# Sources of the output projections transposed in 32x32 blocks by VectorE and reloaded through HBM, TensorE keeping the last ones

## The reference

```python
z = jnp.einsum('btd,de->bte', h, w_in)            # 1024 -> 8192: rq rk rv rg dq dk dv gr gd
y_r = einsum('btv,vd->btd', silu(rg) * rmsnorm(o_ret, g_ret), w_ret_o)
y_d = einsum('btv,vd->btd', rmsnorm(o_att, g_sub) * (1 - lam_init), w_diff_o)
m = sigmoid(gr) * y_r + sigmoid(gd) * y_d
x = x + einsum('btd,de->bte', m, w_out)
x = x + hier_moe(rmsnorm(x, g_ffn), ...)          # 16 experts, 2 per row
```

## Time and profile before

| | |
|---|---|
| median of 3 runs | 1011.21 us (1010.29 to 1013.48) |
| profiled execution | 1012.54 us, its span 1010.4 us |
| PE busy | 990.2 us, 98% |
| DVE busy | 689.5 us, 68% |
| ACT busy | 509.1 us, 50% |
| granted clock of PE | 0.991 |
| transposes under L1834 | 160 |

### The profile page before, as it was taken

One profiled execution on the slowest core, in us unless ns is written; L12 is line 12 of the kernel. 1 busy time (PEld: TensorE's weight loads), 2 busy tenths in 40 slices (PEclk: granted clock), 3 DMA queues, 4 the chain that ended last, 5 costly groups with the idle time before them and its releaser, 6 DMA issues.

```text
span 1010.4 us, 12083 instructions
## 1 busy us (share of the span) xinstructions
PE 990.2 (98%) x4614; PEld 812.8 (80%) x4614; DVE 689.5 (68%) x1003; ACT 509.1 (50%) x680; POOL 149.7 (15%) x184
## 2 busy tenths in 40 slices
PE   9989999999999999999999999999999999999995
PEld 6878888887887888877878888889788888888884
DVE  6699886237656664443448457687889889888893
ACT  6523233335545553332352304554588687887782
POOL 1000001112120301221130000022012122121111
PEclk9999999999999999999999999998999999999998
DMA  9489888882551732553285245137899999999994
GB/s 350 138 250 316 236 222 227 270 247 101 195 192 69 262 114 77 194 204 127 97 299 186 104 152 228 69 127 281 337 401 403 381 404 391 393 405 380 404 397 80
DMA packets 125987, 245.27 MB, mean 243 GB/s; under 512 B 69072, under 2 KB 69376, under 8 KB 113600
## 3 DMA queue, kind: packets, MB, share of 16 engines
q1 hardware_dynamic: 105520, 172.51, 47.1%
q0 software_dynamic: 20112, 71.37, 21.2%
q10 hardware_dynamic: 288, 0.52, 0.1%
HBM read 203.07 MB, written 52.08 MB: 253 GB/s over the span
## 4 chain that ended last, share of the span: by engine, by line
PE 56%; issue 27%; DVE 6%; POOL 3%; SPq 2%; ACT 2%; DMA 1%; POOLq 0%; ACTq 0%; DVEq 0%
PE ps L478 14%; PE ps L480 14%; PE ps L479 14%; PE ps L1861 3%; PE ps L1862 3%; SPq L586 2%; PE ps L1834 2%; POOL x_exp L855 1%; PE ps L1896 1%; POOL out_y L866 1%; PE ps L2004 1%; PE ps L2020 1%; DVE w_lo L450 1%; PE ps L2011 1%; DMA v_tok<-out_v_new 1%
## 5 line engine op out<-in xcount | busy, mean ns | idle before, releaser
L478 PE MATMUL ps<-w_hi,s_hi 128*128 128x512 f32 x640 | 256.4, 401 | 3.1 <-DVE w_lo L414 2.6
L480 PE MATMUL ps<-w_lo,s_hi 128*128 128x512 f32 x640 | 250.3, 391 | 0.0
L479 PE MATMUL ps<-w_hi,s_lo 128*128 128x512 f32 x640 | 249.9, 390 | 0.0
L478 PEld LDWEIGHTS ps<-w_hi,s_hi 128*128 128x128 f32 x640 | 120.6, 188 | 29.2 <-issue 4.6
L479 PEld LDWEIGHTS ps<-w_hi,s_lo 128*128 128x128 f32 x640 | 120.7, 189 | 25.5 <-issue 1.0
L480 PEld LDWEIGHTS ps<-w_lo,s_hi 128*128 128x128 f32 x640 | 120.5, 188 | 25.6
L1013 ACT ACTIVATE stage<-ps,x_rstd 128x512 f32<-128x512 f32 x64 | 43.6, 688 | 150.8 <-PE ps L480 150.4
L414 DVE TENSOR_TENSOR w_lo<-raw,w_hi 128x2048 fp32r<-128x2048 f32 x40 | 91.6, 2290 | 32.2 <-ACT w_hi L409 31.9
L409 ACT CAST w_hi<-raw 128x2048 fp32r<-128x2048 f32 x40 | 76.1, 1908 | 12.0 <-DMA raw<-in_w_in 6.3
L450 DVE TENSOR_TENSOR lo_x<-raw_x,hi_x 128x2048 fp32r<-128x2048 f32 x32 | 72.5, 2286 | 7.9 <-ACT hi_x L427 7.9
L450 DVE TENSOR_TENSOR lo_x<-raw_x,w_hi 128x2048 fp32r<-128x2048 f32 x32 | 72.6, 2286 | 5.4 <-ACT w_hi L427 5.4
(11 more groups left out here) (308 smaller groups left out, 1833.2 us busy)
## 6 DMA issues: line engine op xcount, KB each, us to landing
raw<-in_w_in SPq DMA_DIRECT2D x30, 1024.0 KB, 10.3
raw_x<-in_w_gate SPq DMA_DIRECT2D x30, 1024.0 KB, 24.7
raw_x<-in_w_down SPq DMA_DIRECT2D x18, 1024.0 KB, 24.0
raw_x<-in_w_up SPq DMA_DIRECT2D x16, 1024.0 KB, 21.5
raw<-in_w_up SPq DMA_DIRECT2D x16, 1024.0 KB, 22.4
raw<-in_w_down SPq DMA_DIRECT2D x14, 1024.0 KB, 23.6
x_slots<-in_c_empty SPq DMA_DIRECT2D x4, 2112.0 KB, 11.3
x_exp<-x_slots POOLq DMA_DIRECT2D x16, 528.0 KB, 13.2
```

The costliest lines, as they stand in the source:

```text
L478: nc.tensor.matmul(out, s_h, w_h, start=first, stop=False)
L479: nc.tensor.matmul(out, s_l, w_h, start=False, stop=False)
L480: return nc.tensor.matmul(out, s_h, w_l, start=False, stop=last)
```

## The change

VectorE transposes the sources in blocks of 32x32, SP stores the blocks to a scratch tensor in HBM (src_T) so that the whole is transposed there, and reloads it over the source (od or ro), in the layout of the product's operand. ACT and DVE then split it from there (loaded_hi, loaded_lo), one instruction of 1024 columns each. PE keeps the transposes of source 3's tile 4, and those of x2 for the routing. A tile is stored in four DMAs (tile 4: two), of 128 KB for sources 1 and 2; source 3 is handled in two halves of 512 columns, the first in x = 2 (stores of 64 KB), the second in x = 3, and what is transposed goes to ro. SP reloads source 1 between the weight loads 29 and 30 and between 31 and 32, source 2 between 35 and 36 and between 37 and 38, the first half of source 3 between 39 and 40, the second between the experts' blocks m = 1 and m = 2. A tile of sources 2 and 3 is split two tiles behind the product instead of one.

```diff
+    od_turned = [at("od_turned0", [P, D_MODEL], f32, X + 98304), at("od_turned1", [P, D_MODEL], f32, X + 102400)]
+    ro_turned = [at("ro_turned0", [P, D_MODEL], f32, X + 69120), at("ro_turned1", [P, D_MODEL], f32, X + 73216)]
...
+    src_T = [None] + [scratch(f"src_T{s}", TT * D_MODEL, P) for s in (1, 2, 3)]
...
+    BY_PE = source_unit(3, PT)
+
+    def turned_source(s, t, c0, c1):
+        if s == 3:
+            return ro[:, t, c0:c1]
+        return (od_turned if s == 1 else ro_turned)[t % 2][:, c0:c1]
...
+        def reload_sources(s, ts, n_turned, half=None):
+            c0, c1 = (0, D_MODEL) if half is None else (half * COLS, (half + 1) * COLS)
+            for i, t in enumerate(ts):
+                sp.wait_ge(src_turned, n_turned + i + 1)
+                blocks = turned_source(s, t, c0, c1)
+                columns = src_T[s][t * D_MODEL + c0:t * D_MODEL + c1, :]\
+                    .rearrange("(j a) (q b) -> q a j b", a=BLOCK, q=STRIPS, b=BLOCK)
+                for q in range(STRIPS if t < PT else SAMPLE // BLOCK):
+                    sp.dma_start(columns[q], blocks[q * BLOCK:(q + 1) * BLOCK, :].rearrange("a (j b) -> a j b", b=BLOCK))\
+                        .then_inc(src_stored[t % 2], 16)
+            for t in ts[-2:]:
+                sp.wait_ge(src_stored[t % 2], stored_source(s, t, half or 0))
+            for t in ts:
+                sp.dma_start(source_rows(s, t)[:, c0 // P:c1 // P, :],
+                             src_T[s][t * D_MODEL + c0:t * D_MODEL + c1, 0:P if t < PT else SAMPLE]
+                             .rearrange("(k p) c -> p k c", p=P)).then_inc(rows_in[t], 16)
+
         for n in range(4, N0):
+            if n == BPC * 15:
+                reload_sources(1, (0, 1), 0)
+            if n == BPC * 16:
+                reload_sources(1, (2, 3, 4), 2)
+            if n == BPC * 18:
+                reload_sources(2, (0, 1, 2), TT)
+            if n == BPC * 19:
+                reload_sources(2, (3, 4), TT + 3)
+            if n == BPC * 20:
+                reload_sources(3, (0, 1, 2, 3), 2 * TT, 0)
             dense_load(n)
...
                 elif m < WR:
+                    if m == 2:
+                        reload_sources(3, (0, 1), 2 * TT + PT, 1)
+                        reload_sources(3, (2, 3), 2 * TT + PT + 2, 1)
                     sp.wait_ge(blocks_used, LAST - 2)
...
+        for t in (3, PT):
+            pool.wait_ge(src_stored[t % 2], stored_source(1, t))
         load_gate("gr", 0, 4)
...
+        def loaded_hi(s, t):
+
+            rows = P if t < PT else SAMPLE
+            if s > 1:
+                wait_out(act, 2 * s - 3, t)
+            act.wait_ge(rows_in[t], landed_source(s, t, 1 if s == 3 else 0))
+            nc.scalar.copy(s_hi[:, :, t * P:t * P + rows], source_rows(s, t)).then_inc(shi_ready, 2)
...
-                if x % 2 == 1 and t >= 1:
-                    source_hi(2 + x // 2, t - 1)
-                if x == 2 and t == 0:
-                    source_hi(2, PT)
+                if x % 2 == 1 and t >= 2:
+                    loaded_hi(2 + x // 2, t - 2)
+                if x == 2 and t < 2:
+                    loaded_hi(2, 3 + t)
             lower_half_of(x)
         dense_hi(act, LAST + 1)
+        loaded_hi(3, 3)
         source_hi(3, PT)
...
+        def turn_source(s, t, half=None):
+            c0, c1 = (0, D_MODEL) if half is None else (half * COLS, (half + 1) * COLS)
+            rows = slice(0, P if t < PT else SAMPLE)
+            if s < 3 and t >= 2:
+                dve.wait_ge(src_stored[t % 2], stored_source(s, t - 2))
+            v.transpose(turned_source(s, t, c0, c1)[rows], (od if s != 2 else ro)[rows, t, c0:c1])\
+                .then_inc(src_turned, 1)
...
                 norm_attention((r - 4) // 2)
+                dve.wait_ge(src_ready, (r - 4) // 2 + 1)
+                turn_source(1, (r - 4) // 2)
...
                     gated_ro(t)
+                    if t == 1:
+                        dve.wait_ge(state_stored, 32 * H)
+                    dve.wait_ge(src_ready, TT + t + 1)
+                    turn_source(2, t)
+                if x >= 2 and t < PT:
+                    dve.wait_ge(p_evacuated, TT * x + t + 1)
+                    turn_source(3, t, x - 2)
...
-            if r >= 16:
-                attended_source(r - 16)
-        attended_source(PT)
...
-                if x % 2 == 1 and t >= 1:
-                    next_source(x, t - 1)
-                if x == 2 and t == 0:
-                    next_source(1, PT)
```

More of the change, by code:

```diff
@@ L310, in build @@
     rot_in, ret_in, router_in = sem("rot_in"), sem("ret_in"), sem("router_in")
-    x_in = [sem(f"x_in{t}") for t in range(TT)]
+    rows_in = [sem(f"rows_in{t}") for t in range(TT)]
     x_padded, x_squared, ms_ready, rms_ready = sem("x_padded"), sem("x_squared"), sem("ms_ready"), sem("rms_ready")
@@ L542, in source_bank, with stored_source, landed_source, source_rows @@
         return 5 + u % 2
+    BY_PE = source_unit(3, PT)
[3 more added lines that the diff above has]
+        return (od_turned if s == 1 else ro_turned)[t % 2][:, c0:c1]
+    def stored_source(s, t, half=0):
+        tiles_of = [k for k in range(PT if s == 3 else TT) if k % 2 == t % 2 and k <= t]
+        strips = sum(STRIPS if k < PT else SAMPLE // BLOCK for k in tiles_of)
+        whole = 2 * STRIPS + (SAMPLE // BLOCK if t % 2 == PT % 2 else 0)
+        return 16 * (whole * min(s - 1, 2) + 2 * STRIPS * half + strips)
+    def landed_source(s, t, half=0):
+        return 16 * (s + 1 + half)
+    def source_rows(s, t):
+        rows = P if t < PT else SAMPLE
+        return (od if s != 2 else ro)[:, t, :].rearrange("p (k c) -> p k c", k=KC)[:, :, 0:rows]
     block = nc.Block()
@@ L831, in _ @@
         for t in range(1, TT):
-            pool.wait_ge(src_transposed, source_unit(3, t) + 2)
+            if t < PT:
+                pool.wait_ge(slo_ready, source_unit(3, t) + 2)
+            else:
+                pool.wait_ge(src_transposed, 2)
             load_residual(t)
@@ L966, in source_hi @@
                     .then_inc(shi_ready, 1)
+        def loaded_hi(s, t):
+            rows = P if t < PT else SAMPLE
+            if s > 1:
+                wait_out(act, 2 * s - 3, t)
+            act.wait_ge(rows_in[t], landed_source(s, t, 1 if s == 3 else 0))
+            nc.scalar.copy(s_hi[:, :, t * P:t * P + rows], source_rows(s, t)).then_inc(shi_ready, 2)
         def square_x(t):
-            act.wait_ge(x_in[t], 16)
+            act.wait_ge(rows_in[t], 16)
             if t:
@@ L1149, in _ @@
         square_ro(UNITS - 1)
-        source_hi(1, PT)
+        loaded_hi(1, PT)
         root()
@@ L1303, in source_lo, with loaded_lo @@
                                 hi.bitcast(f32), ALU.subtract).then_inc(slo_ready, 1)
+        def loaded_lo(s, t):
+            rows, c0 = P if t < PT else SAMPLE, t * P
+            dve.wait_ge(shi_ready, source_unit(s, t) + 2)
+            hi = s_hi[:, :, c0:c0 + rows]
+            lo = s_lo[:, :, c0:c0 + rows] if t < PT else s_hi[:, :, c0 + rows:c0 + 2 * rows]
+            v.tensor_tensor(lo, source_rows(s, t), hi.bitcast(f32), ALU.subtract).then_inc(slo_ready, 2)
+        def turn_source(s, t, half=None):
[5 more added lines that the diff above has]
+                .then_inc(src_turned, 1)
         def sum_halves(bank, n):
@@ L1545, in _ @@
             if r >= 16:
-                source_lo(1, r - 16)
-        source_lo(1, PT)
+                loaded_lo(1, r - 16)
+        loaded_lo(1, PT)
         dve.wait_ge(ro_squared, UNITS)
@@ L1616, in _ @@
                     dense_lo(dve, LAST)
-                if x % 2 == 1 and t >= 1:
-                    source_lo(2 + x // 2, t - 1)
-                if x == 2 and t == 0:
-                    source_lo(2, PT)
+                if x % 2 == 1 and t >= 2:
+                    loaded_lo(2 + x // 2, t - 2)
+                if x == 2 and t < 2:
+                    loaded_lo(2, 3 + t)
         def rows_of_tile(t):
@@ L2036, in _ @@
             tile_state(r)
-            if r >= 16:
-                attended_source(r - 16)
-        attended_source(PT)
         def next_source(x, t):
[L2044 to L2047, removed]
+            if x == 3:
                 pe.wait_ge(p_evacuated, TT * x + t + 1)
```

22 lines of the change are left out of this document (10 added, 12 removed).

## The result

| | before | after |
|---|---|---|
| median | 1011.77 us (4 runs) | 1022.68 us (4 runs, 1020.5 to 1027.17) |
| ratio | | 1.011, 95% interval 1.0082 to 1.0138 |
| profiled execution, its span | 1012.54, 1010.4 us | 1027.17, 1025.2 us |

The change makes the kernel 1.1% slower: 1022.68 us against the 1022.5 forecast. The profiled execution is the slowest of the four, so the terms are read between marks inside the trace and not from the two spans.

What follows compares the result with a forecast made beforehand. TensorE's queue of matmuls was taken as the bound. Savings and delays summed to +10.2 us at the half tile of x = 4, plus 1.1 for the clock, +11.3: 1022.5 us from the median, range 1008 to 1032.

Steps and rivals of the forecast that it cites:

- The signs named ahead: Whole kernel: 48 transposes, x = 1 near 541, two TensorE waits (9 and 7 us), stores landing after 10 us, clock below 1.
- Removed, 0.87 a group: TensorE: 14 groups of 8 transposes leave at 0.87 us each, 12.2 us; everything hidden, 13.5 us gained.
- x = 0: First output stage: VectorE's added block transposes of source 2 delay x = 1's first product by 1.0 us; +1.2 carried.
- "Nothing" for late weight loads: x = 1 and x = 2: SP issues two weight loads about 10 us late, used a stage away, so no cost.
- Steps 1 and 2: x = 3: source 3's second-half stores queue behind 7.3 MB; tiles 0 and 1 stored at 619.6, reloaded and split by 626.3.
- Step 3: End of x = 3: VectorE evacuates tile 3 only behind the reloaded tile's lower part; TensorE waits 9.0 us before x = 4.
- Step 4: x = 4 behind tile 0: tile 3's stores and reloads, then the half tile's rows, come late; second TensorE wait, 7.3 us.
- Steps 5 and 6: Behind the second wait: casts and lower parts delay x = 4's half tile to 647.7, +10.2 us; clock fall adds 1.1.
- Stores are not held: Rival, 18 in 100: in x = 3, source 3's stores do not wait behind weight loads; 1017 us, at the least 1008.
- Cost more than their rows: Rival, 15 in 100: stores and reloads dearer than the profile's rows; 1030 to 1034 us, in one place only 1026.
- Hidden: Rival, 14 in 100: source 3 returns in time for x = 4; 1004.6 us, or 997.7 if VectorE is punctual in x = 0.
- The rule of the 19: Rival, 1 in 100: transposing stores 19 times slower, five runs' time more in two chained waits; +31 us, 1053 us.

Runs made afterwards that it cites:

- e9: e8, with source 3's tiles 1 to 3 also going through memory and split in x = 4, TensorE keeping tiles 0 and 4: 1004.83 us, ratio 0.9907.
- e8: e5, with tile 4 of x = 0 evacuated first and source 2 block transposed and reloaded earlier, by pairs: ratio 0.9948 against the kernel before.
- e1: The changed kernel with source 3 transposed by TensorE again, sources 1 and 2 through memory: ratio 0.9988 against the kernel before.
- e2: Only source 1 goes by VectorE and memory; sources 2 and 3 by TensorE as before: ratio 0.9981 against the kernel before.
- e4: The changed kernel with GpSimd, not SP, issuing stores and reloads of source 3's second half: ratio 1.0082 against the kernel before.
- e3: The changed kernel with source 3's second half stored and reloaded ahead of the experts' blocks m = 0 and 1: ratio 1.0058 against the kernel before.
- e7: The changed kernel with the splits of source 3's tiles 0 to 2 behind all other ScalarE and VectorE work of x = 3: ratio 1.0048 against before.
- e10: The changed kernel with e3's earlier stores and the splits of tiles 0 and 1 behind the evacuations of x = 3: ratio 1.0011 against the kernel before.
- e5: e1 with the block transposes of source 2 moved from x = 0 into x = 1: ratio 1.0012 against the kernel before.
- e6: e5, with source 3's tiles 1 to 3 also going through memory and split in x = 4, TensorE keeping tiles 0 and 4: ratio 1.0002.

## Why the prediction was right

The mechanism was right: held stores, evacuations in program order behind reloads, and two waits ended by L1684. That the sum met the median within 0.2 us is luck, for its terms missed by 1 us and more both ways. The signs named ahead came: 48 transposes under L1928, x = 1 at 541.1 (543.85 less the 2.8 us of the late mark), two waits ended by L1684, two stores that landed after more than 10 us, a clock below 1 behind the second wait; only that wait was less than half the size named.

- **Removed, 0.87 a group.** x = 1 to x = 3 is shorter by 3.1 us; five groups of 0.87 are 4.35, and a half clock at the head of x = 1 took about 1.5 back. e9 against e8 has 3 groups, 2.6 us, and measures 3.0 between their medians. Their traces differ by 3.3 us up to the half tile of x = 4, but 1.7 of these are a half clock that e8's has and e9's has not, and a wait of 0.9 that only e9's has goes the other way.
- **x = 0.** Forecast +1.0 us at the first product, measured +0.05 between the marks; the six traces with this code have -0.3 to +1.7, 0.6 in the mean, so that the term is not refuted. Here the gate landed 53.5 us behind the mark, forecast 54.7 (in e1 54.4). That VectorE bounds the stage is shown by e2: minus 3.8 us without the three block transposes. These took 1.25 us, not 1.2.
- **"Nothing" for late weight loads.** TensorE had no wait for a weight in x = 2 or x = 4. w_out's first block is cast at 608.48 instead of 600.17, and tile 1's block transpose stands behind its lower part, at 612.63. In the changed kernel that cost nothing that shows, since SP was at the stores of tile 0 until 618.9; in e4 GpSimd waited for it.
- **Steps 1 and 2, stores behind loads.** Right in mechanism (e3). From the start of x = 3 tiles 0 and 1 are stored at 29.5 us (625.59 less 596.13), forecast 26.3; tile 0's reload landed in 2.7 us, where 4.5 with its issue were put. Two errors of opposite sign.
- **Step 3, the evacuation behind a reload.** Right: an idle time of 10.7 us against 9.0, ended by L1684.
- **Step 4, the second wait.** Mis-sized, 3.3 us instead of 7.3. It ended 46.8 us behind the start of x = 3, forecast 47.3. But TensorE had come 1.7 us later out of the first wait, and its clock in tile 0 was half at first, 0.56 over 4 us: 1.6 more. With the 0.5 us of the earlier end these are the missing 4 us, to 0.2. What it lost to the clock there it did not lose in the wait.
- **Steps 5 and 6, the work behind the second wait and the clock.** From the end of that wait to the half tile of x = 4: forecast 7.1 us and 1.1 for the clock, measured 7.9 (6.5 before). The half clock came there as forecast, 0.52 over 3 us, and cost 1.4 us of work. From the start of x = 3 to the half tile of x = 4 the forecast is 54.4 and 1.1, 55.5 us in all, and the measure 54.6. The clock also fell where the sum had nothing: behind the first wait, where the second swallowed it, and at the head of x = 1. The windows of the first 3.5 us of x = 1, of the first 4 of x = 4 and of the 3 behind the second wait (granted clock, third number from the end):

```profile
543.80:547.30 3.50, 3.45 (x9) 2.82 (x10) 3.32 (x7) 0.00 (x0) 0.00 (x0) 0.57 0.92 150
...
632.00:636.00 4.00, 3.62 (x10) 2.88 (x10) 3.96 (x4) 0.22 (x1) 0.00 (x0) 0.56 0.38 66
...
642.90:645.90 3.00, 3.00 (x12) 2.77 (x13) 2.13 (x3) 2.94 (x3) 0.54 (x1) 0.52 1.02 403
```

So 1022.5 was met with a term of about 1.3 us missing in x = 1 (the clock), 1.1 too many in x = 0 and 0.9 too many from x = 3 to x = 4. The +1.4 us behind the half tile, where the forecast had nothing, were not tested; they are less than the spread of the other traces in that stretch.

- **The rivals.** "Stores are not held" is refuted by e3 and the 9.9 us. "Cost more than their rows" did not show: the reloads of the second half landed in 2.7 to 4.6 us. "Hidden" was wrong for the tile that x = 4 wants first and right for the three it wants late: e9 hides them. The rule of the 19 did not show: stores of the first half of source 3, in runs of 128 bytes, landed within 1.9 us.

## What to carry to other kernels

Moving work from the bound engine to a path through memory pays only for operands with time to spare: count from the last write of the operand to its first use, and put in that time the other engine's pass, two landings, and every byte that stands ahead in the same queue. An instruction that waits for such a reload belongs behind the evacuations that free the bound engine, and the tiles wanted first stay where they were. Here the whole change cost 1.1%; with tile 0 of the third source left on TensorE, and the block transposes moved to where VectorE has slack, it gained 0.9% (e9).

## What the hardware showed unexpectedly

- **A wait of TensorE costs more than its length.** In the traces around these waits, from 480 to 710 us, behind each wait of 2.8 us and more (x = 1: the changed kernel, e1, e3, e4, e7, e10; x = 2: e5; x = 4: the changed kernel, e3 and e4 twice each, e7 and e10 once) the granted clock fell to 0.5 (1.2 GHz of 2.4) for 3 to 6 us, with products 0.43 us apart instead of 0.23; that costs 1.4 to 3.1 us of work. Behind a wait of 2.13 to 2.17 us at the head of x = 1 it stayed at 1.00 in e2, e6 and e9, and fell about a microsecond later in e5 and e8. The Trainium skill (TensorE: Matmul & The Clock Gate, Part 1) has a TensorE that stands idle fall back to the half clock; behind the long waits the traces agree, behind those of 2.1 us only two of five.
- **SP's issue stalls behind large loads.** A store that takes 0.51 us to issue took up to 6.5 us behind 6 MB of loads, and held up everything else in SP's program.
- **A second queue shares the traffic.** GpSimd's stores of tile 0 landed in 5.6 us instead of 9.9 (medians), and its first two reloads in 7.7 and 7.6 instead of 2.7 and 3.1. The Trainium skill (DMA: Bandwidth & Descriptors, Issuing engines are not separate DMA queues) says that issuing from several engines saves only the time of issue, on the same 16 DMA engines; for the reloads the trace agrees, while the stores of tile 0 did land 4 us sooner behind their issue.
